# Per-token normalisation factors, dummy products, later hybrid heads and gates, and looser PSUM waits in a six-layer fp32 transformer stack

## The reference

```
def rms_norm(x, g):
    y = x * lax.rsqrt(jnp.mean(x * x, axis=-1, keepdims=True) + NORM_EPS)
    return y * g
# first block, layer 0 with mixer_ab (attention over picked tokens, and pooling),
# layer 1 with mixer_cd (latent attention, and a gated linear recurrence, "LRU")
    h = rms_norm(x, mix_pre_g[layer])
    m = mixer(h)
    x = x + rms_norm(m, mix_post_g[layer])          # a post norm
    h = rms_norm(x, ffn_pre_g[layer])
    f = channel_mixer(h, ...)                       # up, conv, gelu * val, down
    x = x + rms_norm(f, ffn_post_g[layer])          # a post norm
# second block, layers 0 and 1: four groups of four heads of 128
    h = rms_norm(x, norm_g);  p = split_columns(h @ w_in)
    fox  = forgetting_attention(q, k, v, log_f) * silu(p["fox_g"])
    diff = rms_norm(differential_attention(...), diff_norm_g) * (1.0 - lambda_init)   # a head norm
    diff = diff * silu(p["diff_g"])
    moba = moba_attention(...) * silu(p["moba_g"])
    gla  = rms_norm(gla_chunked(...), gla_norm_g) * silu(p["gla_g"])                  # a head norm
    x = x + concatenate([fox, diff, moba, gla]) @ w_out
```

## Time and profile before

| | |
|---|---|
| median of 3 runs | 2840.71 us (2835.01 to 2843.76) |
| the profiled execution | 2837.55 us, span 2835.7 us |
| TensorE busy | 2749.1 us (97% of the span) |
| DVE, ScalarE, GpSimd busy | 1945.8, 1379.4, 518.3 us (69%, 49%, 18%) |
| mean granted clock of TensorE | 0.99 |

### The profile page before, as it was taken

One profiled execution on the slowest core, in us unless ns is written; L12 is line 12 of the kernel. 1 busy time (PEld: TensorE's weight loads), 2 busy tenths in 40 slices (PEclk: granted clock), 3 DMA queues, 4 the chain that ended last, 5 costly groups with the idle time before them and its releaser, 6 DMA issues.

```text
span 2835.7 us, 50169 instructions
## 1 busy us (share of the span) xinstructions
PE 2749.1 (97%) x18314; PEld 2484.2 (88%) x18314; DVE 1945.8 (69%) x2757; ACT 1379.4 (49%) x1931; POOL 518.3 (18%) x487
## 2 busy tenths in 40 slices
PE   8999999999999999999999999999999999999998
PEld 8998988888888899988888888899878889987887
DVE  6675678777744787678777754676667766666775
ACT  5434555554544557555555444453445454344553
POOL 1150025444411000023444411000000020000001
PEclk9999999999999999999999999999999999999999
DMA  7455445555555455445555555444544555554454
GB/s 253 156 176 182 151 147 178 187 183 187 187 188 185 140 168 164 134 142 171 185 185 185 185 187 186 153 163 161 179 144 149 168 182 173 165 176 143 148 170 141
DMA packets 132569, 482.61 MB, mean 170 GB/s; under 512 B 15040, under 2 KB 15296, under 8 KB 132288
## 3 DMA queue, kind: packets, MB, share of 16 engines
q1 hardware_dynamic: 130608, 475.06, 51.1%
q10 hardware_dynamic: 1808, 5.39, 0.6%
HBM read 477.25 MB, written 2.10 MB: 169 GB/s over the span
## 4 chain that ended last, share of the span: by engine, by line
PE 90%; DVE 5%; ACT 2%; POOL 2%; issue 1%; DMA 0%; DVEq 0%; ACTq 0%; POOLq 0%
PE BANK L462 32%; PE BANK L457 28%; PE BANK L463 16%; PE BANK L478 8%; DVE WLO L1324 1%; PE BANK L839 1%; PE BANK L532 1%; ACT WHI L890 1%; PE BANK L469 1%; PE BANK L829 1%; PE BANK L849 0%; POOL M L2058 0%; DVE TM L1346 0%; PE BANK L676 0%; POOL M L2061 0%
## 5 line engine op out<-in xcount | busy, mean ns | idle before, releaser
L1324 DVE TENSOR_TENSOR WLO<-RING,WHI 128x1024 fp32r<-128x1024 f32 x902 | 1112.9, 1236 | 664.5 <-ACT WHI L890 657.7
L890 ACT ACTIVATE WHI<-RING 128x1024 fp32r<-128x1024 f32 x902 | 954.0, 1059 | 1144.4 <-PE BANK L463 636.2
L462 PE MATMUL BANK<-H,WHI 128*128 128x512 f32 x2560 | 917.8, 403 | 14.7 <-DVE H L1334 9.8
L457 PE MATMUL BANK<-H,WHI 128*128 128x256 f32 x4160 | 764.8, 286 | 22.3 <-DVE H L1334 19.0
L463 PE MATMUL BANK<-H,WLO 128*128 128x256 f32 x2560 | 719.8, 281 | 0.0
L457 PEld LDWEIGHTS BANK<-H,WHI 128*128 128x128 f32 x4160 | 653.2, 193 | 28.9 <-issue 23.2
L462 PEld LDWEIGHTS BANK<-H,WHI 128*128 128x128 f32 x2560 | 483.0, 189 | 136.0 <-issue 15.3
L457 PE MATMUL BANK<-H,WLO 128*128 128x256 f32 x2080 | 590.2, 284 | 0.0
L462 PE MATMUL BANK<-BIGR,WHI 128*128 128x512 f32 x1536 | 539.9, 396 | 3.4 <-DVE BIGR L1957 3.4
L463 PEld LDWEIGHTS BANK<-H,WLO 128*128 128x128 f32 x2560 | 485.5, 190 | 1.7 <-issue 1.0
L463 PE MATMUL BANK<-BIGR,WLO 128*128 128x256 f32 x1536 | 431.0, 281 | 0.0
(11 more groups left out here) (281 smaller groups left out, 2348.3 us busy)
## 6 DMA issues: line engine op xcount, KB each, us to landing
RING<-w SPq DMA_DIRECT2D x902, 512.0 KB, 3.3
X<-xT ACTq DMA_DIRECT2D x4, 512.0 KB, 9.9
outT<-M SPq DMA_DIRECT2D x3, 512.0 KB, 2.9
TB<-tab ACTq DMA_DIRECT2D x1, 1216.5 KB, 5.5
V<-vec ACTq DMA_DIRECT2D x1, 644.0 KB, 8.6
TM<-BIG ACTq DMA_DIRECT2D x16, 32.0 KB
TM<-BIG ACTq DMA_DIRECT2D x8, 64.0 KB
outT<-M SPq DMA_DIRECT2D x2, 256.0 KB, 3.2
```

The source lines that it names most:

```text
L457: last = mm(bank[:, 0:T], wt[s][:, kk, :], x, start=start and n == 0, stop=stop and n == 2)
L462: mm(bank[:, :], WHI[s][:, kk, :], both, start=start, stop=False)
L890: A(WHI[at % SPLIT][:, :, :], RING[at % RAW][:, :].rearrange("p (k n) -> p k n", k=UB), ACT.Copy)\
L1324: TT(WLO[at % SPLIT][:, :, :], RING[at % RAW][:, :].rearrange("p (k n) -> p k n", k=UB), WHI[at % SPLIT][:, :, :].bitcast(f32), ALU.subtra ...
```

## The change

1. Post norms by token. Four matmuls with the squares as the stationary operand and one column of ones moving (`sums_by_token`) give the sum of token t in partition t, 128x2. Mean, root and reciprocal are of 128x2. DVE multiplies ident by the two columns (a diagonal matrix per half, 128x256, TM[:, 11]), and TensorE multiplies ones by it (`spread`), which puts the factor of each token in every partition, in the PSUM bank BANK[o0 % 4]. `lead` reads it from there.
2. Dummy products. `occupy(bank, n)` issues n matmuls ident by ones, 256 columns f32, into a bank that is overwritten next: 2 before and 5 after the spread of a post norm, 7 before RUN_LRU's first product, 6 in `queries`.
3. PSUM waits. run_q's first group waits for output o0-2 instead of o0. In RUN_POOLED and RUN_GATES outputs 0 and 1 wait for o0-4 and the next for o0+1, where each waited for its own number less three.
4. Hybrid layers. gla, diff and moba heads start two units later on all engines, TensorE's diff norm too (103 to 105). There are five gates instead of four, moba in two halves of two tiles; they start at units 98, 113, 115 and 119 (before: gla 98, fox 106, diff 114, moba after the stage), on DVE one unit later, and a second step lies between a gate's two halves of work.
5. Head norms by token: 8 one-column matmuls, mean, root and reciprocal of 128x8, one product 128x1024 for the diagonals, two spreading matmuls of 512 columns, two scalings of 128x512 that read PSUM. The diff heads no longer wait for gla's norm at their start but before their first transposes.

```diff
-        GATE_AT = {"gla": 98, "fox": 106, "diff": 114}
-        def group_out(group):
-            return slice(GROUP_OUT[group], GROUP_OUT[group] + 4)
-        def group_gate(group):
+        GATES = (("gla", 0, 4), ("fox", 0, 4), ("diff", 0, 4), ("moba", 0, 2), ("moba", 2, 4))
+        GATE_AT = (98, 113, 115, 119)
+        MIXED_STARTS = (0, 4, 8, 12, 14)
...
+            def occupy(bank, n):
+                for _ in range(n):
+                    mm(bank[:, 0:T], ident, tcol("ones", T), start=True, stop=True)
...
-                    pe.wait_ge(sem("bank_free"), o0 + 4 * max(quad - 1, 0))
+                    pe.wait_ge(sem("bank_free"), o0 + 4 * (quad - 1) if quad else o0 - 2)
...
+                if u0:
+                    occupy(banks[0], 2)
+                    spread(BANK[o0 % BANKS])
+                    occupy(banks[0], 5)
...
+            def sums_by_token():
+                at = lambda t: BANK[7][:, T + t:T + t + 1]
+                tokens_of = lambda tile, t: TM[:, tile, t * P:(t + 1) * P]
+                pe.wait_ge(sem("sq_added"), 15 * step_no(c, "added"))
+                mm(at(0), tokens_of(4, 0), ones[:, 0:1], start=True, stop=False)
+                pe.wait_ge(sem("sq_done"), 16 * step_no(c, "event"))
+                mm(at(0), tokens_of(3, 0), ones[:, 0:1], start=False, stop=True)
+                mm(at(1), tokens_of(4, 1), ones[:, 0:1], start=True, stop=False)
+                mm(at(1), tokens_of(3, 1), ones[:, 0:1], start=False, stop=True).then_inc(sem("summed"), 1)
+            def spread(bank):
+                pe.wait_ge(sem("diagonal"), step_no(c, "diagonal"))
+                mm(bank[:, 0:T], ones, TM[:, 11, :], start=True, stop=True).then_inc(sem("spread"), 1)
...
-                    if not isinstance(i, int) or o >= BANKS and not (led and i == 1 and j < BANKS - 1):
+                    if r in (RUN_POOLED, RUN_GATES) and isinstance(i, int) and i == 0:
+                        pe.wait_ge(sem("bank_free"), o0 - 4 if j < 2 else o0 + 1)
+                    elif not isinstance(i, int) or o >= BANKS and not (led and i == 1 and j < BANKS - 1):
...
+                                if k == 0:
+                                    occupy(BANK[o0 % BANKS], 7)
...
-                sums()
+                sums_by_token()
...
+                pe.wait_ge(sem("bank_free"), c["output"] - (BANKS - 1))
+                occupy(BANK[c["output"] % BANKS], 6)
...
-            def head_norm(squares, banks):
+            def head_norm(squares, banks, apart):
                 n = step_no(c, "head_norm")
                 pe.wait_ge(sem("head_squared"), n)
+                for at in range(8):
+                    last = mm(banks[0][:, at:at + 1], squares[:, at // 2, at % 2 * P:(at % 2 + 1) * P], ones[:, 0:1],
+                              start=True, stop=True)
+                last.then_inc(sem("head_summed"), 1)
+                yield from rest(apart)
...
-                    pe.wait_ge(sem("head_mean"), 4 * l + 2)
...
+                        if kind == "diff" and h == 0:
+                            pe.wait_ge(sem("head_half"), 4 * l + 2)
...
-                    later(62, heads("fox", l, o0 + 13, o0 + 33)), later(74, gla_heads(l, o0 + 29)),
-                    later(78, heads("diff", l, o0 + 21, o0 + 41)), later(102, heads("moba", l, o0 + 29, o0 + 45)),
-                    later(103, head_norm(M[:, 4:8, :], (BANK[5], BANK[5]))))
+                    later(62, heads("fox", l, o0 + 13, o0 + 33)), later(76, gla_heads(l, o0 + 29)),
+                    later(80, heads("diff", l, o0 + 21, o0 + 41)), later(104, heads("moba", l, o0 + 29, o0 + 45)),
+                    later(105, head_norm(M[:, 4:8, :], (BANK[5], BANK[5]), 10)))
...
-                root(TM[:, 10, :])
+                act.wait_ge(sem("mean_sq"), step_no(c, "rstd"))
+                A(small(ROOT_COL, 2), small(MEAN_COL, 2), ACT.Sqrt).then_inc(sem("root"), 1)
...
-                act.wait_ge(sem("head_mean"), 2 * n)
-                A(squares, squares, ACT.Sqrt).then_inc(sem("head_root"), 1)
+                act.wait_ge(sem("head_mean"), n)
+                A(head_columns(), head_columns(), ACT.Sqrt).then_inc(sem("head_root"), 1)
...
-            def gate(group, l, g0):
-                n = step_no(c, "gate")
-                act.wait_ge(sem("bank_free"), g0 + 4 * (GROUPS.index(group) + 1))
-                z = BIG[:, group_gate(group), :]
+            def gate(n, l, g0):
+                act.wait_ge(sem("bank_free"), g0 + 4 * GROUPS.index(GATES[n][0]) + GATES[n][2])
+                z = BIG[:, gate_z(n), :]
                 A(z, z, ACT.Silu).then_inc(sem("silu"), 1)
                 yield
-                act.wait_ge(sem("gated_heads"), 4 * l + GROUPS.index(group) + 1)
-                A(BIGR[:, group_out(group), :], z, ACT.Copy).then_inc(sem("mixed_hi"), 1)
+                yield
+                act.wait_ge(sem("gated_heads"), len(GATES) * l + n + 1)
+                A(BIGR[:, gate_out(n), :], z, ACT.Copy).then_inc(sem("mixed_hi"), 1)
...
-                    later(62, heads("fox", l)), later(76, gla_heads(l)), later(78, heads("diff", l)),
-                    later(102, heads("moba", l)), later(102, diff_norm(l)),
-                    *(later(at, gate(group, l, o0 + 45)) for group, at in GATE_AT.items()))
+                    later(62, heads("fox", l)), later(78, gla_heads(l)), later(80, heads("diff", l)),
+                    later(104, heads("moba", l)), later(104, diff_norm(l)),
+                    *(later(at, gate(n, l, o0 + 45)) for n, at in enumerate(GATE_AT)))
...
+                if post:
+                    dve.wait_ge(sem("spread"), step_no(c, "spread"))
...
-                            STT(TM[:, 8 + k % 2, :], M[:, k, :], vcol(post[0], KT * post[1] + k), TM[:, 10, :],
+                            STT(TM[:, 8 + k % 2, :], M[:, k, :], vcol(post[0], KT * post[1] + k), BANK[o0 % BANKS][:, 0:T],
...
-                mean(D_MODEL, TM[:, 10, :])
-                reciprocal(TM[:, 10, :])
+                dve.wait_ge(sem("summed"), c["summed"])
+                TS(small(MEAN_COL, 2), BANK[7][:, T:T + 2], 1.0 / D_MODEL, EPS, ALU.mult, ALU.add).then_inc(sem("mean_sq"), 1)
+                dve.wait_ge(sem("root"), step_no(c, "rstd"))
+                then(v.reciprocal(small(RECIP_COL, 2), small(ROOT_COL, 2)))
+                TT(TM[:, 11, :].rearrange("p (a t) -> p a t", a=2), ident.rearrange("p (a t) -> p a t", a=1).broadcast_to([P, 2, P]),
+                   small(RECIP_COL, 2).rearrange("p (a t) -> p a t", t=1).broadcast_to([P, 2, P]), ALU.mult)\
+                    .then_inc(sem("diagonal"), 1)
...
-            def head_norm(values, squares, banks, gain, out, summed):
+            def head_norm(values, squares, banks, gain, out, root_later, spread_later):
                 n = step_no(c, "head_norm")
+                dve.wait_ge(sem("head_summed"), n)
+                TS(head_columns(), banks[0][:, 0:8], 1.0 / P, EPS, ALU.mult, ALU.add).then_inc(sem("head_mean"), 1)
+                yield from rest(root_later)
+                dve.wait_ge(sem("head_root"), n)
+                then(v.reciprocal(head_columns(), head_columns()))
+                TT(flat(squares).rearrange("p (a t) -> p a t", a=8),
+                   ident.rearrange("p (a t) -> p a t", a=1).broadcast_to([P, 8, P]),
+                   head_columns().rearrange("p (a t) -> p a t", t=1).broadcast_to([P, 8, P]), ALU.mult)\
+                    .then_inc(sem("head_diagonal"), 1)
+                yield from rest(spread_later)
                 for half, bank in enumerate(banks):
-                    dve.wait_ge(sem("head_summed"), 2 * n - 1 + half)
-                    TS(squares[:, 2 * half:2 * half + 2, :].rearrange("p a b -> p (a b)"), bank[:, :],
-                       1.0 / P, EPS, ALU.mult, ALU.add).then_inc(sem("head_mean"), 1)
-                    for _ in range(summed):
+                    pair = slice(2 * half, 2 * half + 2)
+                    dve.wait_ge(sem("head_spread"), 2 * n - 1 + half)
+                    STT(flat(out[:, pair, :]), flat(values[:, pair, :]), gain, bank[:, :], ALU.mult, ALU.mult)\
+                        .then_inc(sem("head_half"), 1)
+                    if not half:
                         yield
-                yield
-                dve.wait_ge(sem("head_root"), n)
-                for h in range(4):
-                    last = v.reciprocal(squares[:, h, :], squares[:, h, :])
-                    if h < 3:
-                        yield
-                then(last)
-                STT(out, values, gain, squares, ALU.mult, ALU.mult).then_inc(sem("head_normed"), 1)
-                dve.wait_ge(sem("head_normed"), n)
+                dve.wait_ge(sem("head_half"), 2 * n)
...
-                n = 4 * l + GROUPS.index(group) + 1
-                z, x = BIG[:, group_gate(group), :], BIG[:, group_out(group), :]
-                dve.wait_ge(sem("silu"), n)
```

(21 more changed lines are left out.)

35 lines of the change are left out of this document (23 added, 12 removed).

## The result

| | before | after |
|---|---|---|
| median, us | 2841.47 (2835.01 to 2843.76, 4 runs) | 2809.03 (2800.37 to 2810.44, 4 runs) |
| profiled execution, us | 2837.55 | 2808.78 |
| TensorE busy | 97% | 98% |
| mean granted clock | 0.990 | 0.997 |

The ratio is 0.9883, with a 95% interval of 0.9857 to 0.9909. The forecast was 2807.7. The two profiled executions lie 28.8 us apart, the medians 32.4; the remark on the median, further down, tells what is known of the difference. The granted clock is a share of TensorE's full clock. Cut into 2835 windows of one us, the trace of the kernel before shows it at 1.00 in 2768 and at 0.50 in 46; the other 21, at 0.51 to 0.99, lie where it falls or comes back.

A forecast was written before the change was run, and what follows sets the result against it. TensorE, busy 97% of the span, was taken as the bound; gains of 8.8 + 3.6 + 5.4 + 15.2 = 33.0 us took the 2840.7 median to 2807.7. Range 2799 to 2819; about 8 in 10 within 2798 to 2823.

The forecast's parts named there:

- A, post norms: The four post norms: shorter wait plus a kept clock, less 0.15, gain 2.2 us each, 8.8 in all.
- The chain's 0.75: Each post norm: from the last square's end to the factor 2.7 us instead of 3.48, so 0.75 gained.
- the clock: Behind each post norm's wait: dummies keep TensorE's granted clock up, worth 1.6 us as a mean.
- the second rival: Post norms, queries and LRU: the clock falls despite the dummies, which then overrun the waits; 2832.5 us, chance 0.06.
- B, queries and LRU: Waits at queries and LRU: dummies keep the clock up, data come no sooner; 1.9 us each, together 3.6.
- C, looser waits: Entries of the values, pooled and gates stages: waits for PSUM banks go, 5.4 us gained, bounds 3.5 and 5.5.
- D, hybrid layers: Heads, head norms and output projection of both hybrid layers: 7.6 us gained per layer, 15.2 in all, bounds 7 and 20.
- The projection's wait: Output projection of each hybrid layer: the 1.7 us wait shrinks to about 0.3, gaining 1.4.
- The second spread: The diff norm in each hybrid layer: TensorE waits for DVE to read the first spread, 0.5 us added.
- The one-column products: Head norms on TensorE: eight added per norm cost 1.9 us (1.6 to 2.4), 3.8 for two norms.
- The first rival: Hybrid layers: the head norms' longer chain of crossings eats the whole gain there; 2822.9 us, chance 0.12.
- The third rival, PSUM reads: The lead's 64 scale steps: each 0.06 us slower reading PSUM, 3.8 us lost; 2811.5 us, chance 0.05.

The follow-up runs named there:

- wide-factor kernel: The changed kernel with post norm factors made as before (128x256 reciprocal, read from SBUF) and nine dummies ahead of each lead; ratio to the kernel before 0.9896.
- the one with the filled idle: The changed kernel with extra dummies around the sums of the second, third and fourth post norms; ratio to the kernel before 0.9902.

## Why the prediction was right, and where its steps were off

The time came out 1.3 us from the forecast, by the steps of the sum 28.7 us in the profiles against 33.0. Part by part:

- **A, post norms: 6.8 against 8.8.** The chain's 0.75 is right to 0.03 at the first place (0.72) and the wide-factor kernel gives the same 0.7 back. The mis-sized term is the clock: I took it as kept at all four. It was kept at the first and the fourth (2.36 and 2.04, against 2.2), and fell onto the dummies at the second and third (0.82 and 1.58); at the fourth that was luck, since it fell there in four other profiles, for 0.9 to 1.3 us. I had looked at the idle between sums and lead only, not at the 0.9 and 2.0 us of waiting ahead of the sums, which stood in the trace of before. That is the second rival at two of four places, though the price was smaller than I put it. The stretches of 1.6 to 1.7 us that I took as harmless (the clock is 1.00 behind 1.63 at 441.13 and 1.7 at 2236.93) had full matmuls up to their start; here idle time, one-column products and dummies follow on each other. That this makes the difference is not shown. The chain's sum was right by luck of its parts: the terms as listed add to 2.3 (0.7, three times 0.2, 0.42, 0.43 and 0.15), not to the 2.7 written; from the end of the last square to DVE's first scaling it took 2.76, and the spreading product alone 0.70 instead of 0.43.
- **B, queries and LRU: 1.7 against 3.6.** The queries gave 1.46. LRU gave 0.21 where 1.9 was put. The clock is up there (1.00 over 1141 to 1145, where it was 0.57 over 1146 to 1150), but it turned into a wait: TensorE now comes to the second group of low parts before DVE has made them, so the 24 matmuls that took 4.62 us take 4.19, with 0.98 of waiting among them. The first of them also starts 0.21 later against the short wait behind the queries than before; that is not explained. The rows (TensorE, in order of time; idle before in brackets):

```profile
1136.53 3.19 PE L500 MATMUL BANK<-TB 128*128 128x256 f32 x14
1140.89 0.50 PE L470 MATMUL BANK<-BIGR,WHI 128*128 128x256 f32 x2 [1.17 <-DVE BIGR L1772]
...
1143.55 0.50 PE L470 MATMUL BANK<-BIGR,WHI 128*128 128x256 f32 x2 [0.98 <-DVE BIGR L1772]
```

  The prediction asked what would be late next for the looser waits, but not here: it said "the data come no sooner" of the first tile, and forgot that this holds for those behind it.
- **C, looser waits: about 5.8 against 5.4.** Right, shown by the kernel with that alone.
- **D, hybrid layers: about 16.6 against 15.2.** The layers gave 9.12 and 10.71; less 4.9 that belong to C, and 1.6 that the first one lost to the slower pace of its projection. The projection's wait went from 1.7 to 0.2, as predicted with 0.3. The moba heads' waits went to 0.4 each. The second spread waits 0.18 in each layer, where I had 0.5. The one-column products (x16 is eight of them) and the instruction behind:

```profile
2077.04 1.84 PE L792 MATMUL BANK<-TB,BIG 128*128 128x1 f32 x16
2078.74 0.49 PE L491 MATMUL BANK<-WHI,H 128*128 128x512 f32 x1
```

  1.70 us for eight, 0.2 under the value taken and inside its bounds. That one column can't be slower than 128 was my assumption: it is 0.21 each against 0.20.
- **The first rival** (the gain eaten by the longer chain) didn't come; the chain's steps lie in different units, and the waits for it are 0.4 in total. Of the 8.0 us of waits before the moba heads the schedule alone took 2.4, the narrow root 4.0 more; but as the one-column products cost 3.4 per layer, the head norms by token lose about 0.5 us per layer, and the schedule alone makes the gain. D had the added 3.8 and 0.5 in its sum, but didn't ask how much of the gain the schedule would make without them. And 3.4 of D's gain, the clock behind the gla heads' waits, is there only against executions of the kernel before in which it fell.
- **The third rival, PSUM reads.** The group of the lead's scaling steps:

```profile
L1431 DVE SCALAR_TENSOR_TENSOR TM<-M,V,BANK 128x256 f32<-128x256 f32 x64 | 30.3, 474 | 3.7 <-PE BANK L579 3.7
```

  474 ns from PSUM, where the same steps (L1376) took 480 from SBUF. The 0.06 us a step with which this rival reckoned don't show.
- **The median.** 32.4 us between the medians and 28.8 between the profiles differ by 3.6: the median before lies 3.9 over its profiled execution and the one after 0.3 over its own, both within the slow group of their kernel (2835 to 2844 and 2809 to 2810). Like groups compared, the change is worth 29 us (2838.7 to 2809.3, medians of the groups), 27 (2828.3 to 2801.3) and 26 (2819.4 to 2793.3). That the forecast of 33 met the median so closely is partly luck of the draw.
- **The range.** Its lower end, a gain of 42, is more than the upper bounds of the parts add to (10.4 + 4 + 5.5 + 20 = 39.9).

The projections show the pace too: 60 us in the first and in the second layer of the changed kernel have 342 and 348 matmuls, at a clock of 1.00 in both.

```profile
2245.00:2305.00 60.00, 60.00 (x342) 52.05 (x341) 39.12 (x54) 31.12 (x42) 12.98 (x11) 1.00 0.58 185
2715.00:2775.00 60.00, 60.00 (x348) 52.48 (x347) 36.14 (x44) 31.68 (x45) 14.63 (x11) 1.00 0.61 195
```

Of all versions the one with the filled idle is the fastest by its trace, 2.1 us ahead of the changed kernel; by times alone that can't be told from the groups.
